# Four-layer model on one core: norms at the layer borders in pieces, transposes two tiles ahead of the first projection

## The reference

```python
for l in range(2):
    mod = silu(c) @ w_ada[l] + b_ada[l]
    shift, scale, gate = split(mod, 3)
    h = layernorm(x) * (1 + scale) + shift
    p = h @ w_in[l]                                # 2048 x 3904
    ...                                            # Fourier mixing, latent attention, gates
    x = layernorm(ALPHA * x + gate * (y @ w_out[l]), ln_g[l], ln_b[l])
h = rms_norm(x, even_norm) @ even_w_in             # then pooling, sparse attention
x = x + y @ even_w_out
h = rms_norm(x, odd_norm) @ odd_w_in               # then windowed attention
x = x + y @ odd_w_out
```

## Time and profile before

| | |
|---|---|
| time, median of 3 runs | 1736.81 us (1736.19 to 1740.44) |
| the profiled execution: time / span | 1742.64 / 1740.8 us |
| mean granted TensorE clock | 0.953 of full |
| PE busy | 1525.3 us (88%) |
| DVE busy | 1161.3 us (67%) |
| ACT busy | 687.0 us (39%) |
| DMA | 342.93 MB, mean 197 GB/s |
| chain that ended last | PE 68%, DVE 13%, DMA 9%, ACT 6% |

### The profile page before, as it was taken

How to read it: one execution, slowest core, us unless ns; L and a number is a source line. 1 busy time by engine, 2 the same in 40 slices (tenths; PEclk the granted TensorE clock), 3 DMA queues, 4 the chain that set the end, 5 groups by cost and what they waited for, 6 DMA issues and landing times.

```text
span 1740.8 us, 24874 instructions
## 1 busy us (share of the span) xinstructions
PE 1525.3 (88%) x9679; PEld 1357.9 (78%) x9679; DVE 1161.3 (67%) x1961; ACT 687.0 (39%) x1169; POOL 58.3 (3%) x86
## 2 busy tenths in 40 slices
PE   1667989988993999999994999999998899999998
PEld 1556778887772988899883988789986798888986
DVE  6887757878788663656666458685554648787553
ACT  1222323423332432444433444454443445565442
POOL 3000000000000000000000000000000600000000
PEclk9977999999996999999996999999999799999999
DMA  8787578989783665577564465524565363334563
GB/s 305 263 318 272 192 228 269 312 311 316 261 282 113 207 213 145 182 270 242 181 194 151 125 194 154 149 85 141 175 192 174 110 187 116 110 110 130 171 218 111
DMA packets 184070, 342.93 MB, mean 197 GB/s; under 512 B 28972, under 2 KB 47632, under 8 KB 183184
## 3 DMA queue, kind: packets, MB, share of 16 engines
q1 hardware_dynamic: 179920, 326.88, 58.5%
q0 software_dynamic: 4032, 14.46, 2.4%
HBM read 339.14 MB, written 2.15 MB: 196 GB/s over the span
## 4 chain that ended last, share of the span: by engine, by line
PE 68%; DVE 13%; DMA 9%; ACT 6%; issue 4%; SPq 0%; DVEq 0%; POOLq 0%; POOL 0%; ACTq 0%
PE PM L1257 57%; PE PB L1257 7%; DMA stg<-in_w_in 6%; DVE AC L1730 2%; DVE wlo L1802 2%; ACT whi L1532 2%; ACT AR L1532 2%; DVE X L1730 1%; DMA stg<-in_w_ada 1%; DMA stg<-in_w_out 1%; PE PB L1384 1%; ACT TMP L1532 1%; PE PB L1459 1%; DVE SM L1730 1%; DVE AR L1730 1%
## 5 line engine op out<-in xcount | busy, mean ns | idle before, releaser
L1802 DVE TENSOR_TENSOR wlo<-stg,whi 128x1024 fp32r<-128x1024 f32 (+3 forms) x424 | 499.4, 1188 | 361.1 <-ACT whi L1532 358.4
L1532 ACT ACTIVATE whi<-stg 128x1024 fp32r<-128x1024 f32 (+3 forms) x424 | 431.3, 1024 | 555.7 <-PE PM L1257 327.3
L1257 PE MATMUL PM<-Hh,whi 128*128 128x256 f32 x1824 | 535.9, 294 | 29.8 <-DVE wlo L1802 17.8
L1257 PE MATMUL PM<-Hl,whi 128*128 128x256 f32 x1824 | 524.4, 287 | 0.0
L1257 PE MATMUL PM<-Hh,wlo 128*128 128x256 f32 x1824 | 524.0, 287 | 0.0
L1257 PEld LDWEIGHTS PM<-Hh,whi 128*128 128x128 f32 x1824 | 357.7, 196 | 45.3 <-issue 22.9
L1257 PEld LDWEIGHTS PM<-Hl,whi 128*128 128x128 f32 x1824 | 358.0, 196 | 0.4
L1257 PEld LDWEIGHTS PM<-Hh,wlo 128*128 128x128 f32 x1824 | 357.7, 196 | 0.0
L1257 PE MATMUL PM<-whi,Hh 128*128 128x512 f32 (+1 forms) x704 | 278.8, 396 | 17.0 <-DVE wlo L1802 10.8
L1257 PE MATMUL PM<-wlo,Hh 128*128 128x512 f32 (+1 forms) x704 | 273.3, 388 | 0.0
L1257 PE MATMUL PM<-whi,Hl 128*128 128x512 f32 (+1 forms) x704 | 273.3, 388 | 0.0
(11 more groups left out here) (227 smaller groups left out, 1235.5 us busy)
## 6 DMA issues: line engine op xcount, KB each, us to landing
stg<-in_w_ada SPq DMA_DIRECT2D x192, 512.0 KB, 5.3
stg<-in_w_in SPq DMA_DIRECT2D x112, 512.0 KB, 5.2
stg<-in_even_w_in SPq DMA_DIRECT2D x80, 512.0 KB, 3.7
stg<-in_w_out SPq DMA_DIRECT2D x64, 512.0 KB, 5.6
stg<-in_odd_w_in SPq DMA_DIRECT2D x64, 512.0 KB, 3.7
stg<-in_even_w_out SPq DMA_DIRECT2D x32, 512.0 KB, 4.0
stg<-in_odd_w_out SPq DMA_DIRECT2D x32, 512.0 KB, 4.5
stg<-in_w_in SPq DMA_DIRECT2D x16, 320.0 KB, 4.0
```

The lines of the kernel that those rows point to most:

```text
L1257: return e.matmul(out, l, r, start=start, stop=stop, skip_group_check=True)
L1532: return e.activation(out, x, f, **k)
L1802: e.tensor_tensor(wlo[s["lo"]][:, :, 0:n], stg[s["slot"]][:, :, 0:n], whi[s["hi"]][:, :, 0:n].bitcast(F32), ALU.subtract).then_inc(SEM["lo ...
```

## The change

1. `run` gets a hook `first`, called before `prep`: at a border the norm, the first two of four XN pieces and the transposes of q = 0, 1, 2 are put ahead of the split of job n+3 (n is the layer's first job), which stood ahead of them.
2. XN is written in four pieces of 512 columns on each engine (`normed`). Pieces 2 and 3 come with jobs 1 and 2, the transposes of q+2 with job q (1 to 5), each behind the split of job n+q+3 and ahead of job q's products.
3. After layer 0, the statistics of token tile 0 for layer 1's norm are made by ACT (sum, mean, sum of squared differences, into XN as scratch) while DVE is at token tile 1; DVE's bn_stats covers tile 1 only. After layer 1, the squares are summed in 1024-column pieces. The last operation of `post_norm` per token tile is two of 1024 columns.
4. For q = 0 of every `transposed`, ACT writes `Hh` straight from PSUM with the affine in it; DVE writes `TMP` after that, not before.
5. The first eight jobs of a layer (`fresh`) multiply the high parts of both tiles first, whi and wlo, waiting for `Hh` only, and then `Hl` x whi.
6. In layer 1 the modulation jobs are mixed in from job 6 on, not 4. Layer 0 keeps its order; its XN is in pieces and its q = 0 as in 4.

The diff, cut:

```diff
     def run(self):
         n = len(self.jobs)
         for i in range(n + AHEAD):
+            j = self.jobs[i - AHEAD] if i >= AHEAD else {}
+            if j.get("first"):
+                j["first"]()
             if i < n:
                 self.prep(self.jobs[i])
             if i >= AHEAD:
-                j = self.jobs[i - AHEAD]
                 if j.get("pre"):
                     j["pre"]()
...
+    def normed(self, cs):
+        for c in cs:
+            self.step("xn", c=c, z_free=self.z_free, **self.norm)
+            self.xn[c] = [self.tick("xn0"), self.tick("xn1")]
...
-    def lead(self, pre, layer):
+    def lead(self, first, trans, layer):
...
-        def both():
-            pre()
+        def lead():
+            first()
+            self.normed((0, 1))
+            trans((0, 1, 2))
             begin()
-        self.jobs[n]["pre"] = both
+
+        def more(q):
+            if q < 3:
+                self.normed((q + 1,))
+            trans((q + 2,))
+            if q == 5:
+                self.zw = self.h[KT - 1]
+        self.jobs[n]["first"] = lead
+        for q in range(8):
+            self.jobs[n + q]["fresh"] = True
+        for q in range(1, 6):
+            self.jobs[n + q]["pre"] = lambda q=q: more(q)
...
-        self.interleave(n1 + 4, ex, 72, 32)
+        self.interleave(n1 + 6, ex, 70, 32)
...
@@ tensor, mm
+                    for kk in range(2) if s["h_hi"] else ():
+                        k = 2 * s["q"] + kk
+                        q.wait_ge(s["h_hi"][kk])
...
+                            for W in (H, L):
+                                w = W[:, kk, u["c0"]:u["c0"] + u["n"]]
+                                if u["kind"] == "A":
+                                    mm(b[0:u["n"], u["off"]:u["off"] + S], w, Hh[:, k, :], first and W is H, False)
...
+                    for kk in range(2) if s["h_hi"] else ():
+                        k = 2 * s["q"] + kk
+                        q.wait_ge(s["h"][kk])
...
+                                ins = mm(b[0:u["n"], u["off"]:u["off"] + S], w, Hl[:, k, :], False, k == KT - 1)
...
@@ scalar, trans
+                    if s["q"] == 0:
+                        q.wait_ge(s["mm"])
+                        q.wait_all(s["need"])
+                        q.wait_ge(s["h_free"])
+                        for k in range(2):
+                            pin = B[:, k * S:(k + 1) * S]
+                            if s["how"] == "mod":
+                                ins = act(Hh[:, k, :], pin, ACT.Identity, bias=MOD[:, k:k + 1], scale=MOD[:, 16 + k:17 + k])
...
@@ scalar, post_norm of layer 0
+                    q.wait_ge(s["out"][1])
+                    act(XN[:, 0, :], X[:, 0, :], accum_out=sm(s["sum"], 1)).then_inc(SEM["pn_sum"], 1)
+                    q.wait_ge(s["summed"])
+                    act(sm(s["nm"], 1), sm(s["sum"], 1), scale=-1.0 / D).then_inc(SEM["pn_mean"], 1)
+                    q.wait_ge(s["mean"])
+                    act(XN[:, 0, :], X[:, 0, :], ACT.Square, bias=sm(s["nm"], 1), accum_out=sm(s["sq"], 1)).then_inc(SEM["pn_sq"], 1)
+                elif kind == "post_norm":
+                    q.wait_ge(s["z_free"])
+                    for n in range(4):
+                        t, cols = n // 2, slice(1024 * (n % 2), 1024 * (n % 2) + 1024)
+                        q.wait_ge(s["out"][n])
+                        act(XN[:, t, cols], X[:, t, cols], ACT.Square, accum_out=sm(s["ss"] + n, 1)).then_inc(SEM["sumsq"], 1)
...
@@ vector, trans and ln
+                        if s["q"] == 0:
+                            q.wait_ge(s["hh"])
...
-                    for t in range(2):
+                    for t in (1,) if s["post"] else (0, 1):
                         for g in range(4):
                             a = seen(e.bn_stats(STA[:, t, g, :], X[:, t, g * 512:(g + 1) * 512]))
...
-                        stt(X[:, t, :], X[:, t, :], y[:, t:t + 1], ar(D, D), ALU.mult, ALU.add).then_inc(SEM["post_norm"], 1)
+                        for o in (0, 1024):
+                            x = X[:, t, o:o + 1024]
+                            stt(x, x, y[:, t:t + 1], ar(D + o, 1024), ALU.mult, ALU.add).then_inc(SEM["post_norm"], 1)
```

More of the change, by code:

```diff
@@ L85, in __init__ @@
         self.x = {}
+        self.xn = [None] * 4
+        self.norm = None
         self.mod = {}
@@ L90, in __init__ @@
         self.ar = ()
-        self.mm_last = self.ln = self.later = self.pool_mm = self.toep = None
+        self.mm_last = self.ln_in = self.later = self.pool_mm = self.toep = None
         self.ss = None
@@ L311, in post_norm, with ln @@
-    def post_norm(self, l):
[L312 to L316, removed]
-            for t in range(2):
[L318 to L324, removed]
+    def ln(self, x, post=None):
+        s = dict(mv=self.small(4), v=self.small(2), y=self.small(2), nb=self.small(1), t=self.small(2), nbt=self.tick("nb"))
+        self.step("ln", x=x, post=post, **s)
+        self.norm = dict(how="ln", ready=s["nbt"], y=s["y"], mv=s["mv"], nb=s["nb"], nm=post["nm"] if post else None)
@@ new lines, in rms, with mod_h @@
+    def rms(self, sst, ss, nss):
+        y, yt = self.small(2), self.tick("rms_y")
+        self.step("rms", sst=sst, ss=ss, nss=nss, v=self.small(2), y=y, t=self.small(2), yt=yt)
+        self.norm = dict(how="rms", ready=yt, y=y)
+    def normed(self, cs):
+        for c in cs:
+            self.step("xn", c=c, z_free=self.z_free, **self.norm)
+            self.xn[c] = [self.tick("xn0"), self.tick("xn1")]
+    def mod_h(self, l, qs):
+        self.transposed("mod", l, qs)
+        self.mod_free = self.h[2 * qs[-1]]
@@ new lines, in post_norm @@
+    def post_norm(self, l):
+        tk = [self.tick("post_norm") for _ in range(4)]
+        s = dict(l=l, ln=self.ln_in, x=self.x[1, 3], mv=self.small(4), v=self.small(2), y=self.small(2), t=self.small(2),
+                 z_free=self.z_free, out=tk)
+        if l == 0:
+            s.update(sum=self.small(1), nm=self.small(1), sq=self.small(1))
+            s["summed"], s["mean"], s["squared"] = self.tick("pn_sum"), self.tick("pn_mean"), self.tick("pn_sq")
+        else:
+            s["ss"] = self.small(4)
+            for _ in range(4):
+                s["squared"] = self.tick("sumsq")
+        self.ar = (tk[3],)
@@ L325, in post_norm @@
         self.h_free = self.mm_last
-        return tk, ss, sq
+        return self.step("post_norm", **s)
     def gate_post(self, blocks):
```

139 lines of the change are left out of this document (79 added, 60 removed).

## The result

The changed kernel takes 1724.66 us (median of 6 runs, 1719.52 to 1729.31) against 1738.95 us for the kernel before in the same session (6 runs, 1736.19 to 1742.13): the medians differ by 14.3 us. The ratio of the two kernels' runs is 0.9912, 95% interval 0.9887 to 0.9937, which is 15.3 us less (11.0 to 19.7). The forecast was 16.0 us less. The profiled execution took 1726.91 us, span 1725.1, which is 15.7 us under the span before.

What follows compares the result with a forecast made beforehand. PE was taken to set the pace between borders, a serial DVE and ACT chain at them. Borders 1, 2 and 3 gain 7.1 + 5.5 + 3.4 = 16.0 us, taking the median 1736.81 to 1720.8 us, range 1713 to 1728.

Steps and rivals of the forecast that it cites:

- The chain to the first product, borders 1 and 2: DVE and ACT's serial work before each border's first product: shortened, so that product starts 10.7 and 9.0 us earlier.
- Step (f): Border 1: ACT writes Hh for q = 0 from PSUM in 1.0 us; PE is ready at about the same time.
- Transposes between products: Border 1, also charged at border 2: twenty transposes formerly ahead of the first product now lie between products, costing 2.3 us.
- The cold start: Borders 1 and 2: the first 1.8 to 3.9 us of products run at half clock, losing 1.2 us each.
- The fit for piece 2: Border 1: XN's piece 2, queued behind a split, just fits PE's need; 0 to 0.4 us lost, 0.1 taken.
- its own list of signs: What would show the forecast, including PE without gaps over 0.5 us in the first group of layers 1 and even.
- Border 3: DVE, not PE, is late; group ends 5.4 us earlier, 2 us lost at kn_bc: 3.4 us gained, bounds 0 and 8.
- Clock from the products: Rival at all borders: the clock starts counting only at the products, 2.6 us lost in all, 1723.4 us; chance 0.10.
- Splits hold the chain: Rival at borders 1 and 2: queue steps take 1 us more per job, 10 us less gain, 1730.8; chance 0.08.
- Border 3 gives all back: Rival: border 3's whole gain is lost again in k_norm, 1724.2 us; chance 0.10.
- The slower one, no clock in a border's group: Rival: waits keep PE at half clock throughout, 1760 us; guard: shortest standstill that lowered it was 3.5 us; chance 0.03.
- Bank of q = 0: Not-as-said case: PE needs that bank before q = 2's transposes, 1.7 us lost per border, 1725.9 us; chance 0.03.

Runs made afterwards that it cites:

- e4: The changed kernel with the split of job n+3 back ahead of the norm and the lead; 1733.04 us (one run).
- e3: The changed kernel with DVE making both token tiles' statistics for the second norm at border 1, without ACT's part; 1729.78 us (one run).
- e11: The changed kernel with q = 0 as before: DVE's affine into TMP first, ACT rounding Hh from it; 1723.84 us (one run).
- e7: The changed kernel with 28, 26 and 40 unread identity transposes on PE ahead of the lead's transposes at borders 1, 2, 3; 1723.3 us (6 runs).
- e2: The changed kernel with all eight q transposed and all four XN pieces written ahead of the first product; 1728.35 us (4 runs).
- e8: The changed kernel with unread warming transposes on PE at the borders and POOL's mask additions moved to the odd layer's third group; 1705.36 us (4 runs).
- run 24: Not a follow-up run: the text says PE had run 24 products of one moving column each, in the kernel before.

## Why the prediction was right, point by point

- **The chain to the first product, borders 1 and 2** (10.7 and 9.0 us forecast): 10.1 and 8.3. XN begins 3.1 us earlier at border 1, not 3.5. The split gives 1.0, not 1.2 (e4); the statistics 2.5, not 2.4 (e3); the halved operations and the small ones that join ACT's sums cost DVE some 0.4, not 0.1. Two XN pieces take ACT 1.52 us, 0.76 each for the 0.73 of the line. Step (f) held that PE is ready when `Hh` is, with the eight further transposes at 0.175 us each; in the row of twelve each takes 0.21 to 0.23 us at half clock, and PE comes 0.3 us after `Hh`. What `Hh` from PSUM saves is mostly behind that (e11: 0.5 us).
- **Transposes between products** (g, 2.3 us): held, five times 0.44 us at full clock:

The chain of waits of the changed kernel at border 2 (start, duration, what):
```profile
938.88 0.44 PE PB L1403 x4
```
- **The cold start** (h, 1.2 us at each): half clock for 1.0 and 3.5 us after the first product, 0.4 and 1.5 us. The mean, 1.0, is near the forecast; the term is a chance, not a constant. The prediction gave 1.8 to 3.9 us for the rise, and border 1 lies outside it.
- **The fit for piece 2** (0.1 us): 0.76 at border 1. The prediction named this place as the one without slack, and put the whole rival at 10 us; it is one job's wait, not five. By its own list of signs a gap over 0.5 us was not to be. How large it is hangs on the clock: in e3 and e4, where the clock at border 1 rose 3.5 and 3.0 us after the first product, PE did not wait there.
- **Sum at borders 1 and 2**: 10.1 - 2.2 - 0.4 - 0.8 = 6.7, measured 6.54; 8.3 - 2.2 - 1.5 = 4.6, measured 4.63. Forecast 7.1 and 5.5.
- **Border 3** (3.4 us): 2.04 at the first group and again 2.05 at the second `kn_bc`. The first product came 7.5 us earlier (8.0). The mis-sized term is DVE's chain beside POOL. From the end of q = 2's `Hl` to the end of the last one it took 17.0 us (1338.78 to 1355.82), where 15 were forecast. Counted from start to start, the chain held six `wlo` of 1.14 us and not five of 1.2 (0.8 us more), an XN piece took 0.87 and not 0.5 (0.7 us for two), and an odd `Hl` 1.14 and not 1.0 (0.4 us for three). Besides, q = 2's `Hl` came 0.7 us later than chained up, and two more `wlo` stand in DVE's queue ahead of the read-out (1355.75), which comes 2.2 us after the last `Hl`. (The prediction's own terms put that `Hl` at 1366.4, not 1366.7.) So the group gains 2.0 us, not 5.4. The wait at the first `kn_bc` grew by 1.1 us as forecast in kind (2 in size), and the second `kn_bc` had it back. PE's longest wait was 3.04 us for an XN piece, not some 2 us for `Hl` or `Hh`.
- **The rest**: 13.2 us by the borders against 16.0 forecast. The timed difference of 15.3 us (11.0 to 19.7) covers both; what the changed kernel has beyond its borders was not shown to come from the change, and in the profiles 1.7 us gained and 1.6 us lost there are falls of the clock. So the mechanism held term by term, but that the total came so near the forecast is in part luck: the borders fell short of it by 0.6, 0.9 and 1.4 us.
- **Rivals.** Clock from the products: refuted by e7, and already by the earlier trace rows, as the prediction said. Splits hold the chain: one wait of 0.76 us. Border 3 gives all back: of the 5.4 us that were expected at its group 2.0 came, and what is missing was never gained there rather than lost in `k_norm`. The slower one, no clock in a border's group: did not happen, but its guard was wrong. In e2 the clock fell between pauses of at most 1.14 us, in the changed kernel itself at 1354.2 after a wait of 1.94 us, and the trace of before had shown shorter ones than 3.5 us: a fall at 1125.0, 1.4 us after a standstill of 1.99 us, and one with no pause at all (last section). Bank of q = 0: PE did not wait there.

## What to carry to other kernels

When a serial border is shortened, ask what else runs beside the chain that is left: here POOL's masks ran beside DVE before and after, but after the change DVE's chain was all that bound the group. Moving the masks to a stretch that PE bounds was worth 11.5 us of that border, and 13 us by the medians, nearly as much as the change; the kernel before would have gained 7.8 us. Read an edit by the length of the stretch it touches, from an event just ahead to one just behind; that mostly repeats to 0.3 us where the span scatters by several, and where it does not, look at the granted clock first: in two unchanged stretches each further fall went with 0.5 to 1.7 us more. And where a stretch begins at half clock, warm PE before comparing variants, since the moment of the rise moves by more than such edits are worth.

## What was not expected of the hardware

The clock does not fall by the length of one pause alone. PE stood 3.04 us at border 3 of the changed kernel and kept full clock (four transposes at 0.63 us behind it), while it lost it in e8 after 1.86 us (the same four at 1.04 us), and in e2 without a pause over 1.14 us. In e8 a wait of 0.43 us stood shortly before; in e2 PE was busy for 0.36, 0.85 and 0.01 of three successive microseconds. The closest pair is e11: at the same place PE stood 3.05 us, and 1.5 us later its clock fell. And in the kernel before it fell at 613.0 with no pause over 0.15 us in the 6 us ahead; there PE had run 24 products of one moving column each. PE's timeline and clock slice of e11, then those of the kernel before:

```profile
1337.28 0.63 PE L1403 MATMUL PB<-IDN,Z 128*128 128x128 f32 x4 [3.05 <-DVE Z L1940]
```
```profile
1338.00:1339.00 1.00, 1.00 (x10) 0.86 0.71 236
```
```profile
610.27 2.73 PE L1257 MATMUL PB<-ONE,AR 128*128 128x1 f32 x24
```
```profile
613.00:614.00 1.00, 1.00 (x4) 0.50 0.81 205
```

What decides between these cases was not tested.
